# A streaming encoder step on one core: more products on split weights, gates and norm reordered, a fifth fixed expert

## The reference, cut to what matters

```python
def mixer_branch(h, ...):
    z = h @ w_in + b_in                       # 1024 x 6144
    a, uv = z[..., :2048], z[..., 2048:4096]
    gates = sigmoid(z[..., 4096:])
    a = glu(a)
    a_full = concatenate([conv_hist, a], axis=1)
    a = silu(layer_norm(depthwise_causal_conv(a_full, conv_w, conv_b), ln_g, ln_b))
    u, v = split(gelu(uv))
    v = layer_norm(v, v_ln_g, v_ln_b)
    y_b = spatial_gate(u, v, w_s, b_s) @ w_b
    merged = gates[..., :1024] * (a @ w_a) + gates[..., 1024:] * y_b
    return merged @ w_o, new_hist, v
# block: mod = silu(c) @ w_ada + b_ada  -> sh1, sc1, g1, sh2, sc2, g2
#   h = rms_norm(x)*(1+sc1)+sh1;  x = x + g1*mixer(h)
#   h = rms_norm(x)*(1+sc2)+sh2;  x = x + g2*hier_moe(h)
# hier_moe: best of 4 groups, best 2 of its 8 experts (32 in all), SwiGLU 1024 -> 256 -> 1024
# final: rms_norm(x) with a shift and scale from silu(c) @ w_ada_f + b_ada_f
```

## Time and profile before

| | us |
|---|---|
| median of 3 runs (lowest, highest) | 961.87 (961.79, 967.13) |
| the profiled execution: its own time | 963.13 |
| its span, first to last instruction | 961.3 |
| busy: PE, DVE, ACT, POOL | 846.9, 516.0, 189.0, 166.2 |
| mean granted TensorE clock | 0.939 |
| A begins on PE; DVE's convolution stream begins | 38.0; 71.0 |
| the convolution stream ends | 269.8 |
| centring ends, the second `mix` begins | 313.4 |
| gates end | 410.3 |
| branch products begin; end | 414.5; 543.5 |
| last full projection ends; the sample's ends | 603.0; 611.0 |
| last router row read by DVE | 624.7 |
| first expert product begins | 660.3 |

### The profile page before, as it was taken

One profiled execution on the slowest core, in us unless ns is written; L12 is line 12 of the kernel. 1 busy time (PEld: TensorE's weight loads), 2 busy tenths in 40 slices (PEclk: granted clock), 3 DMA queues, 4 the chain that ended last, 5 costly groups with the idle time before them and its releaser, 6 DMA issues. The chain is left out here.

```text
span 961.3 us, 12080 instructions
## 1 busy us (share of the span) xinstructions
PE 846.9 (88%) x4970; PEld 615.2 (64%) x4970; DVE 516.0 (54%) x752; ACT 189.0 (20%) x281; POOL 166.2 (17%) x156
## 2 busy tenths in 40 slices
PE   3899999999997979979999999917999988878776
PEld 1588886347996979968878644705666655445532
DVE  1429999999999542352375443481333331222235
ACT  3211211011242121831220011201111110101003
POOL 1000000000046263143123000002122221121110
PEclk9999999999998889989999999857999998989889
DMA  9922314012323112265999693243999999999925
GB/s 338 320 63 71 88 46 173 1 44 79 87 62 96 37 52 63 70 220 179 331 313 321 184 379 140 114 176 105 412 404 414 416 417 396 377 412 391 372 107 225
DMA packets 109592, 204.16 MB, mean 212 GB/s; under 512 B 9548, under 2 KB 68276, under 8 KB 100318
## 3 DMA queue, kind: packets, MB, share of 16 engines
q1 hardware_dynamic: 91184, 159.36, 46.8%
q10 hardware_dynamic: 12830, 34.93, 9.5%
q0 software_dynamic: 5520, 9.06, 2.6%
HBM read 199.49 MB, written 14.84 MB: 223 GB/s over the span
## 5 line engine op out<-in xcount | busy, mean ns | idle before, releaser
L1277 DVE SCALAR_TENSOR_TENSOR arena<-arena,VT 128x574 f32<-128x574 f32 x240 | 175.1, 808 | 0.0
L860 PE MATMUL PS<-arena 128*64 128x256 f32 (+1 forms) x1056 | 147.0, 407 | 29.8 <-issue 25.6
L860 PEld LDWEIGHTS PS<-arena 128*64 128x64 f32 (+1 forms) x1056 | 106.6, 155 | 65.6 <-issue 37.7
L1692 POOL TENSOR_TENSOR wL<-arena,wH 128x1024 fp32r<-128x1024 f32 x32 | 81.0, 2556 | 348.6 <-ACT wH L996 348.5
L553 PE MATMUL PS<-arena 128*128 128x272 f32 x512 | 119.3, 396 | 0.3 <-DMA arena<-w_in 0.3
L553 PEld LDWEIGHTS PS<-arena 128*128 128x128 f32 x512 | 98.2, 192 | 21.2 <-DMA arena<-w_in 0.6
L620 PE MATMUL PS<-gH,wH 128*128 128x272 f32 x384 | 82.6, 297 | 9.2 <-POOL wL L1692 5.5
L1588 DVE TENSOR_TENSOR arena<-PS,arena 128x256 f32<-128x256 f32 x19 | 8.1, 424 | 138.1 <-ACT arena L1112 138.1
L620 PE MATMUL PS<-gL,wH 128*128 128x272 f32 x384 | 81.7, 295 | 0.0
L620 PE MATMUL PS<-gH,wL 128*128 128x272 f32 x384 | 81.2, 293 | 0.0
L880 PE MATMUL PS<-arena 128*64 128x512 f32 (+1 forms) x264 | 69.1, 597 | 1.4 <-DVE arena L1592 1.4
(11 more groups left out here) (280 smaller groups left out, 1004.7 us busy)
## 6 DMA issues: line engine op xcount, KB each, us to landing
arena<-w_gate SPq DMA_DIRECT2D x32, 1024.0 KB, 10.5
arena<-w_up SPq DMA_DIRECT2D x32, 1024.0 KB, 16.6
arena<-w_down ACTq DMA_DIRECT2D x28, 1024.0 KB, 14.7
arena<-w_in SPq DMA_DIRECT2D x40, 512.0 KB, 5.2
arena<-w_ada SPq DMA_DIRECT2D x8, 1024.0 KB, 18.5
vecs<-w_ada SPq DMA_DIRECT2D x4, 2048.0 KB, 10.1
arena<-w_ada SPq DMA_DIRECT2D x4, 2048.0 KB, 9.3
arena<-x_prompt SPq DMA_DIRECT2D x8, 512.0 KB, 8.6
```

Of the source, the lines that this page charges most:

```text
L860: last = pe.matmul(PS[h * rows:(h + 1) * rows, 2, n * DE:(n + 1) * DE], hG[:, b, k * SLOTS + h * rows:k * SLOTS + (h + 1) * rows], buf[r / ...
L1277: dve.scalar_tensor_tensor(out=total, in0=src, scalar=tap, in1=total, op0=ALU.mult, op1=ALU.add).then_inc(conv_step, 1)
L1692: pool.tensor_tensor(wL2[q % 2][:, m], WP[q % 2][:, m], wH2[q % 2][:, m], ALU.subtract).then_inc(gw_split, 1)
```

## The change

- A's units 2 to 7, V and the output projection use the split form. ACT makes the high parts (`high_a`, `high_v`, `high_o`, `high_m`), DVE the low ones (`low_a`, `low_v`, `low_o`, `low_m`), A's and V's inside the convolution. gH and gL are made before the convolution. A's weights use four buffers instead of two. V and the projection treat the sample as a fifth token tile in each half.
- V's norm is ten scalar_tensor_tensor instructions on DVE; POOL has no part in it. The square root for it stands on ACT behind gate 3. The squares go from POOL to ACT, behind gate 10.
- PE runs gates 0 to 5 ahead of the mixing, and the sum over features behind gate 3 instead of gate 1.
- A modulation unit is now two rows of k for 2048 columns instead of eight for 512, so that DVE adds three times (128 partitions) instead of 48 times, and there are three groups of stores.
- The projection takes the token tiles in the order 0, 1, 2, 4, 3.
- Expert 4 is fixed too, in a buffer of its own in `vecs` and `spare`, loaded behind the router rows. The other fixed experts are loaded after the projection (0 and 1 were loaded ahead of its end). The lone tiles among 3 to 12 are the even ones instead of the odd ones, and the placement arithmetic on DVE has one more small instruction.

```diff
-NSTATIC, NWIDE = 4, 5
+NSTATIC, NWIDE = 5, 5
 NDYN = NE - NSTATIC
-NPAIR = (NDYN - NWIDE + 1) // 2
+NPAIR = (NDYN - NWIDE + 2) // 2
...
-        wH2 = [split_parts(f"wH2{s}", O_W + 4096 * s + 2048, 2, KT, P) for s in range(2)]
-        wL2 = [split_parts(f"wL2{s}", O_W + 4096 * s, 2, KT, P) for s in range(2)]
+        A_AT = (O_W, O_W + 4096, O_U, O_V)
+        wHA = [split_parts(f"wHA{s}", at + 2048, 2, KT, P) for s, at in enumerate(A_AT)]
+        wLA = [split_parts(f"wLA{s}", at, 2, KT, P) for s, at in enumerate(A_AT)]
+        wH2, wL2 = wHA[0:2], wLA[0:2]
...
+        ringed = [view(O_A + 6144 * r, 3, KT, DE) for r in range(4)]
+        first_gu = vecs[:, 0:2 * KT * DE].rearrange("p (m k n) -> p m k n", m=2, n=DE)
+        WG = [r[:, 0] for r in ringed] + [first_gu[:, 0]]
+        WU = [r[:, 1] for r in ringed] + [first_gu[:, 1]]
+        WD = [view(O_A + 6144 * r + 4096, 2, D) for r in range(4)] + [spare[:, :, :]]
...
         for t in range(1, ALWAYS + 1):
             first = in_tile[-1][-1] + 1 if t > 1 else 0
-            alone = 2 < t <= 2 + 2 * NWIDE and t % 2 == 1
+            alone = 3 < t <= 2 + 2 * NWIDE and t % 2 == 0
             again = t == 4
-            in_tile.append([first] if alone else [first - again, first + 1 - again])
+            in_tile.append([first - again] if alone else [first, first + 1])
...
+        def place_of(n):
+            return n if n < NSTATIC else (n - 1) % 4
+
+        def before_it(n):
+            return n - 5 if n < NSTATIC + 4 else n - 4
...
+                    if n < FIRST_FP32:
+                        last = product(4 * b + 2 * m, WA[n % 4][:, m], hT, first=(n == 0))
+                    else:
+                        pe.wait_ge(w_low, 2 * (n - FIRST_FP32) + m + 1)
+                        last = product_split(4 * b + 2 * m, wHA[n % 4][:, m], wLA[n % 4][:, m], gH, gL)
...
+                for part in (gH, gL):
...
+            gate(2)
+            gate(3)
             pe.wait_ge(conv_sum, 1)
             pe.wait_ge(hist_copied, 2)
             over_features(6, rstdc)
-            gate(2)
-            gate(3)
+            gate(4)
+            gate(5)
...
-                gate(4 + h // 2)
-            for j in range(8, 12):
+                gate(6 + h // 2)
+            for j in range(10, 13):
...
+                for k in range(2):
+                    for q in range(4):
+                        last = pe.matmul(PS[NSAMPLE * q:NSAMPLE * (q + 1), 4 + g % 2, :], cT32[:, k0 + k, :], AW[b][:, k, q * BLK:(q + 1) * BLK],
+                                         start=(k0 + k == 0), stop=(k0 + k == KT - 1))
...
+            def project_high(t, hf, first=False):
+                w, bank = WIDTH[t], (2 * t + hf) % 8
+                for k in range(KT):
+                    if first:
+                        pe.wait_ge(m_high, k + 1)
+                    pe.matmul(PS[0:w, bank, :], mH[:, k, place_of_rows(t)], wHO[hf][:, k, :], start=(k == 0), stop=False)
+                for k in range(KT):
+                    if first:
+                        pe.wait_ge(m_split, k + 1)
+                    pe.matmul(PS[0:w, bank, :], mL[:, k, place_of_rows(t)], wHO[hf][:, k, :], start=False, stop=False)
...
+            pe.wait_ge(w_high, OW_HIGH + 2)
+            pe.wait_ge(dve_drained, KT + NGATE - 1)
+            project_high(0, 0, True)
+            pe.wait_ge(dve_drained, KT + NGATE)
+            project_high(1, 0)
+            pe.wait_ge(w_low, OW_LOW + 2)
+            project_low(0, 0)
+            project_low(1, 0)
...
             load_first(3)
+            for p in range(2):
+                sp.wait_ge(mod_stored[p], (128, 64)[p])
+            sp.wait_ge(log_ps, 1)
+            load_first(4)
...
+                if n < 4:
+                    high_a(n + 4)
+                if n == 5:
                     act.wait_ge(bias_split, 3)
-                if n in (2, 3, 4, 5):
...
-            act.wait_ge(v_var, 1)
-            act.activation(vsd[:, 0:4], mv[:, 0:4, 1], ACT.Sqrt, bias=eps[:, :])
-            act.activation(vsd[0:NSAMPLE, 4:5], mv[0:NSAMPLE, 4, 1:2], ACT.Sqrt, bias=eps[0:NSAMPLE, :]).then_inc(v_sd, 1)
...
+                if j == 3:
+                    act.wait_ge(v_var, 1)
+                    act.activation(vsd[:, 0:4], mv[:, 0:4, 1], ACT.Sqrt, bias=eps[:, :])
+                    act.activation(vsd[0:NSAMPLE, 4:5], mv[0:NSAMPLE, 4, 1:2], ACT.Sqrt, bias=eps[0:NSAMPLE, :]).then_inc(v_sd, 1)
...
+                if j == KT + 2:
+                    act.wait_ge(mix_ps, KT)
+                    act.wait_ge(v_stored, 16)
+                    act.wait_ge(centred, KT)
+                    for n in range(KT):
+                        act.activation(sq[:, n, :], cv[:, n, :], ACT.Square).then_inc(squared, 1)
...
+            def low_a(i):
+                for m in range(2):
+                    dve.wait_ge(w_high, 2 * (i - FIRST_FP32) + m + 1)
+                    dve.tensor_tensor(wLA[i % 4][:, m], WA[i % 4][:, m], wHA[i % 4][:, m], ALU.subtract).then_inc(w_low, 1)
+
+            def low_v(hf):
+                for k in range(0, KT, 4):
+                    dve.wait_ge(w_high, VW_HIGH + 2 * hf + k // 4 + 1)
+                    dve.tensor_tensor(wLW[hf][:, k:k + 4, :], W[hf][:, k:k + 4, :], wHV[hf][:, k:k + 4, :], ALU.subtract).then_inc(w_low, 1)
+
+            low_a(2)
+            low_a(3)
...
-                    if i == 6 and k in (9, 17, 25):
-                        low_u((k - 1) // 8)
-                if i == 2:
-                    dve.wait_ge(g_high, KT)
-                    for j in range(KT):
-                        dve.tensor_tensor(gL[:, j, :], hT[:, j, :], gH[:, j, :], ALU.subtract).then_inc(g_split, 1)
-                if i == 4:
-                    low_u(0)
+                    if i == 0 and k in (6, 14, 21, 28):
+                        low_a((6, 14, 21, 28).index(k) + 4)
+                    if i == 2 and k in (6, 20):
+                        low_v(k // 20)
+                    if i == 4 and k in (18, 27):
+                        low_u(k // 27)
...
-                ins = dve.tensor_scalar(vt, vt, mv[0:w, t, 0:1], vsd[0:w, t:t + 1], ALU.subtract, ALU.mult)
-                if t >= 3:
-                    ins.then_inc(v_scaled, 1)
-                    continue
-                then(ins)
-                then(dve.tensor_tensor(vt, vt, vgb[0:w, :], ALU.mult))
-                dve.tensor_tensor(vt, vt, vbb[0:w, :], ALU.add).then_inc(v_norm, 1)
...
+                soon(dve.scalar_tensor_tensor(out=vt, in0=vt, scalar=mv[0:w, t, 0:1], in1=vgb[0:w, :], op0=ALU.subtract, op1=ALU.mult))
...
+                dve.scalar_tensor_tensor(out=vt, in0=vt, scalar=vsd[0:w, t:t + 1], in1=vbb[0:w, :], op0=ALU.mult, op1=ALU.add).then_inc(v_norm, 1)
...
+            def add_bias(g):
+                b = g % 2
+                dve.wait_ge(bias_in[b], 64 * (g // 2 + 1))
+                if g == 2:
+                    dve.wait_ge(mod_stored[0], 64)
+                dve.wait_ge(mod_ps, 4 * g + 4)
...
+                if j in (7, 11):
+                    add_bias(j // 4 - 1)
+                if j == NGATE - 2:
+                    for n in range(KT - 3):
+                        low_m(n)
+            for n in range(KT - 3, KT):
+                low_m(n)
+            low_o(0)
+            add_bias(2)
+            low_o(1)
 
...
-            pool.wait_ge(mix_ps, KT)
-            pool.wait_ge(v_stored, 16)
-            for j in range(KT):
-                pool.wait_ge(centred, j + 1)
-                pool.tensor_tensor(sq[:, j, :], cv[:, j, :], cv[:, j, :], ALU.mult).then_inc(squared, 1)
```

More of the change, by code:

```diff
@@ L1061, in _ @@
             for half in range(2):
-                gate(KT + 4 + half)
+                if half:
+                    gate(KT + 5)
                 for j in range(4 * half, 4 * half + 4):
@@ L1127, in load_later @@
                     at = 2 * (t - 1) + h
[L1128 removed]
+                    load_d(at if i is None else i * 2 + at, later(t)[h][0])
             def expert_tile(i, t, b):
```

465 lines of the change are left out of this document (248 added, 217 removed).

## The result

The kernel became slower by 0.4%: 967.42 us (median of 12 runs) against 963.0 us for the kernel before (12 runs beside them), ratio 1.0043, 95% interval 1.0025 to 1.0061. The forecast was 949. The profiled execution took 968.5 us with a span of 966.8 (before 963.13 and 961.3).

| from, to | before | after | difference | forecast |
|---|---|---|---|---|
| start, DVE's convolution stream begins | 71.0 | 72.9 | +1.9 | 0 |
| stream begins, gates end | 339.3 | 343.2 | +3.9 | +1.7 |
| gates end, branch products begin | 4.2 | 5.6 | +1.4 | 0 |
| branch products | 129.0 | 127.7 | -1.3 | -1.5 |
| products end, last router row read | 81.2 | 85.2 | +4.0 | -5.7 |

A forecast was written before the change was run, and what follows sets the result against it. DVE's convolution stream was taken to bound up to the gates, then PE, then arriving expert weights. Terms +1.7 - 1.5 - 5.7 - 7.4 = -12.9 from 963.1 gave 950.2, less 1.3 for the median: 949; range 934 to 959.

The forecast's parts named there:

- DVE's stream: DVE's convolution stream: added subtractions +18.2 us, gL's moved ahead -5.1, so it ends 13.1 later, at 282.9.
- rival of dear subtractions: DVE's subtractions in its stream cost more than 1.14 us per 1024 elements; up to 999 us, chance 0.05.
- None of these 26 us is booked: A and V: PE's 26 us saved count for nothing, since u needs its low parts from DVE.
- From the stream to the mixing: DVE's stream end to the mixing, called the decisive place: centring 21.3 us later, gates' end +1.7 after savings.
- If they take turns, each puts 2.35 us on DVE: Inside DVE's stream: POOL's four subtractions for gates 0 to 3 add +9.4 us, stream end 292.3.
- POOL is shut out as long as DVE's tap stream runs: Rival for DVE's tap stream: gate 0 waits until 285.7, norm ends at 332.4; 951 us, chance 0.18.
- it costs nothing here: ACT's square root behind gate 3: gate 3 ends at 298, before DVE's statistics, so no cost.
- Branch products: Modulation additions: forty-eight on two partitions become three of 128, saving PE's one wait; -1.5 us, bounds 0 and -3.
- Projection and router: Output projection to last router row: split matmuls -8.4 us, tile 0's norm +1.5, tail +1.2; sum -5.7.
- covers all but what it waits today: Projection start: PE's 7.2 us of high-part work hides DVE's forming of low parts, adding no wait beyond the present one.
- Experts: Expert tiles: loads behind the routing fall from 28 to 27; -7.4 us, bounds -9 and 0.
- may leave DMA idle: Expert loads: after the first buffers reopen, 1, 2, 1 loads per tile instead of 2, 1, 2 may idle DMA.

The follow-up runs named there:

- e12: The changed kernel with DVE's taps of the last pair chained one by one from tap 18 on; ratio 1.0011 to the kernel before, -3.1 us against the changed kernel.
- e5: The changed kernel with the output projection as a float32 product again; ratio 1.0122 to the kernel before, +7.6 us against the changed kernel.
- e2: The changed kernel with the low weight parts of gates 0 to 3 formed by DVE instead of POOL; ratio 0.9957 to the kernel before.
- e9: The changed kernel with four fixed experts and the lone tiles and placement of the kernel before; ratio 1.0063 to the kernel before.
- e4: The changed kernel with A and V as float32 products again, u's low parts left in place; ratio 1.0138 to the kernel before.
- e7: The changed kernel with A and V in float32 and u's low parts placed as in the kernel before; ratio 0.9940 to the kernel before.

## Why the prediction was wrong

**DVE's stream.** Right. It was the bound; it ended at 284.5, forecast 282.9; subtractions cost 1.14 us per 1024 elements; u's first low part came at 211.8 (211), u ended near 272.6 (271.5); PE stood 10.9 us before u (13). V ended at 202.2, not 197. The rival of dear subtractions is out: a pair takes 2.36 us as before. "None of these 26 us is booked" was right: V ended 20.7 us earlier and u 1 us earlier.

**From the stream to the mixing.** The failed step is "If they take turns, each puts 2.35 us on DVE". They did not. It was the rival "POOL is shut out as long as DVE's tap stream runs", with chance 0.18: gate 0 waits to 285.7 (measured 286.8), gate 3 ends at 314.5 (315.7), the norm at 332.4 (334.8). The row for it had been read, POOL waiting past two taps, and I gave it less weight than the 2.84 us addition. Additions follow each other with a gap (one each 0.79 us, of 0.76), the taps overlap, and e12, which changes nothing but the chaining of the taps, shows that this is what decides. The sum moved little, since either engine's waiting cost about the same here: +3.9 instead of +1.7, and 1.4 more at the branch start, where POOL also meets a cast (not in the forecast). That the two cases lay so close was luck. The rival had been sized loosely too: its norm, 3.1 us later than the forecast's, would give +4.8 and 952, where +2.7 and 951 were written. Nor did "it costs nothing here" hold for ACT's square root: behind the late gate 3 it made DVE wait 11.6 us.

**Branch products.** -1.3, forecast -1.5: right.

**Projection and router.** The largest miss, +4.0 for -5.7. The matmuls were nearly right: 0.231 us for 0.226, -7.1 for -8.4. The failed step is that PE's high-part work at the start "covers all but what it waits today": it looked at DVE and priced nothing for ACT, whose high part, 3.7 us, stands between the landing of w_o and PE's first matmul. +3.6 of waiting, +2.2 of half clock behind it. e5, without that high part, waits 1.7 us there. Tile 0's norm cost +1.5 as forecast (PE waits 2.3 us ahead of its turns, 0.8 before). The tail was +3.1 for +1.2, but this size belongs to the clock: the forecast's 14.9 us were 16.8 in after, 12.4 in e2 with the same instructions.

**Experts.** -5.7 for -7.4, inside its bounds, and e9 gives 5.5 for the fifth expert; the gap that "may leave DMA idle" is there (0.67 for 10 us is 3.3 us). +1.2 before it is a first tile at half clock (9.45 for 8.49).

The forecast's sum was -12.9 and the table's is +5.4, 18.3 us apart. Projection and router are 9.7 of these; without that miss the time would have been near 958, inside the range of 934 to 959. The rest is the gates 2.2, the start 1.9, the experts 1.7, the branch start 1.4, the stretch ahead of the first load 1.2 and the branch products 0.2. Of the 9.7, 5.8 are ACT's high part with the half clock behind it, 1.9 the tail, 1.3 the matmuls and 0.7 not accounted for. So the range failed for one reason above all. Each stretch had been given a cost on the engine that I had named as its bound, and the new high parts on ACT were only checked where ACT had idle time on average.

## What to carry to other kernels

In this kernel a POOL subtraction beside DVE's two-input taps wasn't slowed but kept out for as long as the stream had no gap (21.01 us for 2.37); give such small work to DVE itself (1.14 us against POOL's 2.37 here), or put it where DVE idles. When PE's work is made cheaper by work on other engines, look for the last of that work between a load's landing and PE's first matmul, since PE has nothing else to do there (3.6 us of waiting here). And in an order written by hand, an experiment that undoes work must undo the places chosen for it as well (e4, e7: 19 us apart).
